# S5 parameter loads beside the output projection, weight slots by time of last use, and the S5 gate ahead of the second half of layer 1's norm

## What is computed

```python
for l in range(2):
    sh1, sc1, g1, sh2, sc2, g2 = split(silu(c) @ ada_w[l] + ada_b[l])   # 1024 x 6144 weights
    h = rms_norm(x) * (1 + sc1) + sh1
    if l == 0:                     # z = h @ w_in (1024 x 3368); A: differential attention, 4 heads
        y = concat(A(z), B(z)) @ w_out                 # B: top-64 sparse attention with an indexer
    else:                          # z = h @ w_in (1024 x 2048); C: causal attention, 8 heads
        s = gelu(s5_scan(u, lam, B, C, D, log_dt))     # D: S5 state-space layer on u, 512 channels
        y = concat(C(z), s * sigmoid(s @ glu_w + glu_b)) @ w_out
    x = x + g1 * y
    h = rms_norm(x) * (1 + sc2) + sh2
    x = x + g2 * hier_moe(h)       # 4 groups, top-2 of 32 experts; w1, w3, w2 of all experts are read
```

## Time and profile before

| | |
|---|---|
| median of 3 runs | 1529.83 us (1529.28 to 1530.37) |
| the profiled execution | 1531.76 us, span 1530.0 us |
| busy: PE, DVE, ACT, POOL | 86%, 28%, 14%, 7% |
| layer 0's mixer, routing included | 0 to 309.57 us |
| layer 0's experts | 309.57 to about 786 us |
| layer 1's mixer, routing included | to 1046.1 us |
| layer 1's experts and output | to the end |
| HBM read | 489.25 MB |

### The profile page before, as it was taken

The page is one execution under the profiler, slowest core; times in us unless marked ns, Lnnn a source line. Parts: engine busy times, 40 slices in busy tenths (PEclk is TensorE's granted clock), DMA queues, the critical chain, the costliest instruction groups (busy, mean ns, idle before and its releaser), DMA issues.

```text
span 1530.0 us, 15107 instructions
## 1 busy us (share of the span) xinstructions
PE 1322.5 (86%) x6157; PEld 662.5 (43%) x6157; DVE 431.4 (28%) x888; ACT 217.9 (14%) x458; POOL 105.6 (7%) x128
## 2 busy tenths in 40 slices
PE   5889989699989988988967865978999899899897
PEld 2334468544334433433435323875343343343333
DVE  3164663721111111110135715253211111111112
ACT  1123241111101110110100004211111010110100
POOL 1110000300300300300000000000000000000000
PEclk8999959699999999999988977779999999999999
DMA  9998521159999999999991097113999999999993
GB/s 371 222 371 344 205 125 55 55 213 430 428 429 427 427 429 427 429 427 428 428 399 63 1 377 310 49 61 116 420 428 428 428 428 426 428 428 428 428 427 159
DMA packets 51801, 493.46 MB, mean 323 GB/s; under 512 B 4744, under 2 KB 5968, under 8 KB 20880
## 3 DMA queue, kind: packets, MB, share of 16 engines
q1 hardware_dynamic: 48816, 488.33, 76.8%
q0 software_dynamic: 1056, 0.89, 1.2%
q10 hardware_dynamic: 1856, 3.20, 0.6%
HBM read 489.25 MB, written 3.15 MB: 322 GB/s over the span
## 4 chain that ended last, share of the span: by engine, by line
PE 48%; DMA 39%; DVE 7%; issue 2%; ACT 2%; SPq 1%; DVEq 0%; POOLq 0%; POOL 0%; PEldq 0%; ACTq 0%
DMA ring<-in_moe_w 34%; PE B L735 19%; PE B L572 5%; PE A L652 4%; PE B L752 3%; PE B L585 3%; DMA ring<-in_ev_w_in 2%; PE B L707 2%; PE B L529 2%; DMA ring<-in_ada_w 2%; PE A L762 2%; PE B L518 2%; PE B L622 1%; PE B L951 1%; DVE work L1030 1%
## 5 line engine op out<-in xcount | busy, mean ns | idle before, releaser
L735 PE MATMUL B<-ring,work 128*64 128x512 f32 x2048 | 475.4, 618 | 62.6 <-DMA ring<-in_moe_w 60.3
L735 PEld LDWEIGHTS B<-ring,work 128*64 128x64 f32 x2048 | 159.5, 142 | 340.5 <-issue 339.1
L752 PE MATMUL B<-ring,work 128*64 128x512 f32 x1024 | 231.8, 594 | 1.2 <-ACT work L1678 1.2
L1301 DVE TENSOR_TENSOR work<-work,B 64x512 f32<-64x512 f32 x64 | 68.1, 1065 | 506.8 <-ACT work L1674 506.3
L752 PEld LDWEIGHTS B<-ring,work 128*64 128x64 f32 x1024 | 75.9, 137 | 137.2 <-issue 137.2
L1674 ACT ACTIVATE work<-B 64x512 f32<-64x512 f32 x64 | 37.7, 589 | 621.5 <-PE B L735 621.5
L762 PE MATMUL A<-work 128*128 128x256 f32 x512 | 118.1, 384 | 8.9 <-DVE work L1307 8.9
L1885 POOL COPY work<-work 128x512 f32 x62 | 38.2, 617 | 1106.3 <-PE B L735 744.8
L762 PEld LDWEIGHTS A<-work 128*128 128x128 f32 x512 | 94.6, 190 | 28.5 <-issue 16.9
L572 PE MATMUL B<-ring,hT 128*128 128x512 f32 (+1 forms) x224 | 96.8, 593 | 5.6 <-DVE hT L1081 3.3
L1307 DVE COPY work<-B 64x512 f32<-64x512 f32 x64 | 43.7, 684 | 117.4 <-PE B L752 117.4
(11 more groups left out here) (248 smaller groups left out, 940.5 us busy)
## 6 DMA issues: line engine op xcount, KB each, us to landing
ring<-in_moe_w SPq DMA_DIRECT2D x192, 2048.0 KB, 19.9
ring<-in_ada_w SPq DMA_DIRECT2D x24, 2048.0 KB, 20.5
ring<-in_ev_w_in SPq DMA_DIRECT2D x6, 2048.0 KB, 22.0
ring<-in_od_w_in SPq DMA_DIRECT2D x4, 2048.0 KB, 19.4
ring<-in_ev_w_out SPq DMA_DIRECT2D x2, 2048.0 KB, 8.1
ring<-in_od_w_out SPq DMA_DIRECT2D x2, 2048.0 KB, 11.0
s_tables<-hT ACTq DMA_DIRECT2D x8, 256.0 KB, 9.5
ring<-s_tables SPq DMA_DIRECT2D x1, 2048.0 KB, 24.6
```

The costliest lines, as they stand in the source:

```text
L735: ins = pe.matmul(B5[64 * m:64 * m + 64, :], xs[:, k, :], w[:, k, :], start=(k == 0), stop=(k == KD - 1))
L752: ins = pe.matmul(B7[64 * m:64 * m + 64, :], hidTb[:, q % 2, k, :], w[:, k, 512 * m:512 * m + 512], start=(k == 0), stop=(k == KF - 1))
L1301: dve.tensor_tensor(hid[64:128, q % 2, :].rearrange("p (k q) -> p q k", k=KF), silu_a[64:128, q % 2, :].rearrange("p (q k) -> p q k", k=KF ...
```

## The change

1. **Slots.** `stream()` gives a load the slot whose content is used first, with "tab" ranked behind ("in", 3). Eight loads of layer 1's mixer get another predecessor, whose use they wait for: ada 7: ("in", 1) in place of tab; ("in", 3): ada 4 (was ("in", 1)); ada 8: ada 5 (ada 4); ada 9: ("in", 2) (ada 5); ada 10: ada 6 (("in", 2)); ada 11: ada 7 (ada 6); glu: ("in", 3) (ada 7); out 1: tab (("in", 3)). All others keep theirs.
2. **S5 loads.** log_dt is read as one row with the norm gains and broadcast by two small matmuls; lam follows it on GpSimd's queue. The router weights of a layer are issued when its last output projection weights have landed, and B, C, D and glu_b after layer 0's last transposes ahead of attention (A3).
3. **S5 matrices.** The DVE block is now the function `s5_matrices`, called between `out_rows_a` and `residual` of layer 0; the seven passes on PE (`s5_transposes`) and ACT stand between `out_proj(0, 0)` and `moe(0)`. The buffers moved accordingly.
4. **Layer 1's gate.** Gelu is y times sigmoid of twice the argument (one DVE op less), and it and the gate stand ahead: DVE does `s5_rows(3)` and gelu's argument, then `c_norm(0)`, the product `gy`, `c_norm(1)`; PE does the gate matmul after tile 0's transposes, then tile 1's, then all of attention; ACT does gelu's sigmoid, root 9, tile 0's copies, root 10, the gate's sigmoids, tile 1's copies.

```diff
+def used_rank(n):
+
+    return N_MIX1 + LOADS1.index(("in", 3)) + 0.5 if n == N_MIX1 + LOADS1.index(("tab",)) else n
+
+
 def stream():
 
 
     slot, fill, old, last, count = [], [], [], {}, [0] * RING
     for n in range(N_ALL):
-        s = n % RING
+        s = n if n < RING else min(last, key=lambda x: used_rank(last[x]))
...
-                 "ada0r2", "bt0", "bt1", "bt2", "bt3", "ct0", "ct1", "k0", "ada0c2", "B0", "B1", "B2", "B3", "ada1r0", "A0", "A1", "A2", "A3"]
+                 "ada0r2", "ada0c2", "B0", "B1", "B2", "B3", "ada1r0", "A0", "A1", "A2", "A3"]
...
-        ORDER += ["oB0", "oB1", "oA0", "oA1", "h0_0", "h0_1", "h0_2", "h0_3", "ada1r1", "ada1c1", "ada1r2", "ada1c2",
+        ORDER += ["oB0", "oB1", "oA0", "oA1", "bt0", "bt1", "bt2", "bt3", "ct0", "ct1", "k0", "h0_0", "h0_1", "h0_2", "h0_3", "ada1r1", "ada1c1", "ada1r2", "ada1c2",
...
+                for g in range(2):
+                    ins = pe.matmul(A4[64 * g:64 * g + 64, 2, 0:16], ones[0:1, 0:64], prow[:, PROWS - 32 + g:PROWS:2], start=True, stop=True)
...
+            def s5_transposes():
+
+                for v in range(4):
+                    tr_unit(f"bt{v}", [Bd[:, v, 4 * q4:4 * q4 + 4, :].rearrange("p a b -> p (a b)") for q4 in range(4)],
+                            [(p5_bt, 1)])
+                for v in range(2):
+                    tr_unit(f"ct{v}", [Cd[:, v, q4, :] for q4 in range(4)])
+                direct_term()
...
                 if q == 4:
-                    for v in range(4):
-                        tr_unit(f"bt{v}", [Bd[:, v, 4 * q4:4 * q4 + 4, :].rearrange("p a b -> p (a b)") for q4 in range(4)],
-                                [(p5_bt, 1)])
-                    for v in range(2):
-                        tr_unit(f"ct{v}", [Cd[:, v, q4, :] for q4 in range(4)])
-                    direct_term()
                     ada_columns(0, 2)
...
+            s5_transposes()
             moe(0)
...
-            def gate(j):
-                if j != GATE_AT:
-                    return
-                for h in range(2):
-                    tr_unit(f"C{2 + h}", [z1[:, 1, 512 * h + P * b:512 * h + P * b + P] for b in range(4)], [(qk_ready, 8)])
+            def gate():
                 n = n_of(1, "glu")
                 pe.wait_ge(gy_ready, 1)
                 full(n)
@@ -995,10 +1001,12 @@
                 ins.then_inc(glu_done, 1)
                 pe.wait_ge(glu_done, 1)
                 pe.nop().then_inc(slot_used, 1)
-                pe.wait_ge(tr_ev, U["C3"] + 1)
-
-            pe.wait_ge(tr_ev, U["C1"] + 1)
-            attention(1, N0, L1_UNITS, gate)
+
+            gate()
+            for h in range(2):
+                tr_unit(f"C{2 + h}", [z1[:, 1, 512 * h + P * b:512 * h + P * b + P] for b in range(4)], [(qk_ready, 8)])
+            pe.wait_ge(tr_ev, U["C3"] + 1)
+            attention(1, N0, L1_UNITS)
...
+            def s5_matrices():
+
+                dve.wait_ge(in_s5, 16 * N_S5)
...
+                tell(p5_bt)
...
             out_rows_a(1, 16)
+            s5_matrices()
             residual(0, 0)
...
-            c_norm(0)
             s5_rows(3)
             dve.wait_ge(y5_read, 4)
 
             w0 = vv[:, 0]
             tt(w0, y5, y5, ALU.mult)
             ts(w0, w0, 0.044715, 1.0, ALU.mult, ALU.add)
-            dve.tensor_tensor(w0, w0, y5, ALU.mult).then_inc(tanh_in, 1)
+            dve.tensor_tensor(w0, w0, y5, ALU.mult).then_inc(gelu_in, 1)
+            c_norm(0)
+            dve.wait_ge(gelu_out, 1)
+            dve.tensor_tensor(gy, w0, y5, ALU.mult).then_inc(gy_ready, 1)
             c_norm(1)
-            dve.wait_ge(tanh_out, 1)
-            ts(w0, w0, 0.5, 0.5, ALU.mult, ALU.add)
-            dve.tensor_tensor(gy, w0, y5, ALU.mult).then_inc(gy_ready, 1)
...
+            act.wait_ge(par_rows, 1)
+            act.activation(s5p[:, 2, :], A4[:, 2, 0:16], ACT.Exp).then_inc(p5_dt, 1)
...
             norm_root(1)
+            for v in range(4):
+                tr_evac(f"bt{v}", BT[:, v // 2, v % 2], 4)
+            for v in range(2):
+                tr_evac(f"ct{v}", CT[:, v], 4)
+            tr_evac("k0", K0[:, :, :].rearrange("p a b -> p (a b)").unsqueeze(1), 1)
             moe(0)
...
+            act.wait_ge(gelu_in, 1)
+            act.activation(vv[:, 0], vv[:, 0], ACT.Sigmoid, scale=2.0 * GELU_C).then_inc(gelu_out, 1)
             root(9, small[:, 0:16])
-            for t in range(TT):
-                if t:
-                    act.wait_ge(tanh_in, 1)
-                    act.activation(vv[:, 0], vv[:, 0], ACT.Tanh, scale=GELU_C).then_inc(tanh_out, 1)
-                    root(10, small[:, 0:16])
-                for h in range(2):
-                    tr_evac(f"C{2 * t + h}", qkT1[:, 4 * h:4 * h + 4, P * t:P * t + P], 4)
-            def gate(j):
-                if j == GATE_AT + 1:
-                    act.wait_ge(in_late, 16 * N_LATE)
-                    act.wait_ge(glu_done, 1)
-                    for f in range(4):
-                        ins = act.activation(vv[:, 1, f, :], OB[f // 2][:, TOK * (f % 2):TOK * (f % 2) + TOK], ACT.Sigmoid, bias=glub[:, f:f + 1])
-                    ins.then_inc(sig_ready, 1)
-
-            attention(N0, L1_UNITS, sc_sb1, prob1, PT1, gate)
+            for h in range(2):
+                tr_evac(f"C{h}", qkT1[:, 4 * h:4 * h + 4, 0:P], 4)
+            root(10, small[:, 0:16])
+            act.wait_ge(in_s5, 16 * N_S5)
+            act.wait_ge(glu_done, 1)
+            for f in range(4):
+                ins = act.activation(vv[:, 1, f, :], OB[f // 2][:, TOK * (f % 2):TOK * (f % 2) + TOK], ACT.Sigmoid, bias=glub[:, f:f + 1])
+            ins.then_inc(sig_ready, 1)
+            for h in range(2):
+                tr_evac(f"C{2 + h}", qkT1[:, 4 * h:4 * h + 4, P:2 * P], 4)
+
+            attention(N0, L1_UNITS, sc_sb1, prob1, PT1)
...
-            pool.wait_ge(h_ready, 2)
+            for dst, src, slow in LAM_PARAMS:
+                pool.dma_start(dst, src, allow_slow_non_contiguous=slow).then_inc(in_lam, 16)
+
+            def router_parameters(l):
+
+                n = n_of(l, "out", 0)
+                pool.wait_ge(slot_full[slot(n)], fills(n))
+                for dst, src, slow in ROUTER_PARAMS[l]:
+                    pool.dma_start(dst, src, allow_slow_non_contiguous=slow).then_inc(in_router[l], 16)
+
+            router_parameters(0)
+            pool.wait_ge(tr_ev, U["A3"] + 1)
             for dst, src, slow in S5_PARAMS:
                 pool.dma_start(dst, src, allow_slow_non_contiguous=slow).then_inc(in_s5, 16)
-            pool.wait_ge(z_ready, 6)
-            for dst, src, slow in LATE_PARAMS:
-                pool.dma_start(dst, src, allow_slow_non_contiguous=slow).then_inc(in_late, 16)
...
+                else:
+                    router_parameters(1)
```

More of the change, by code:

```diff
@@ L624, in att_pv, with attention @@
                 ins.then_inc(pv_done, 1)
-            def attention(l, base, units, hook):
+            def attention(l, base, units, hook=None):
                 n = len(units)
@@ L866, in _ @@
                     ada_rows(0, 1)
-                    tr_unit("lam", [s5row[:, :]], [(in_s5, 16 * N_S5)])
+                    tr_unit("lam", [s5row[:, :]], [(in_lam, 16 * len(LAM_PARAMS))])
                 if q == 2:
@@ L1651, in att_pt, with attention @@
                 tr_evac(f"p{base + j}", pt[:, (base + j) % 2, 0:nb, :], nb)
[L1653 removed]
+            def attention(base, units, buf, pr, pt, hook=None):
                 n = len(units)
```

104 lines of the change are left out of this document (48 added, 56 removed).

## The result

The changed kernel takes 1484.95 us (median of 4, 1482.93 to 1486.34) against 1529.55 us (4 runs, 1528.52 to 1530.37): ratio 0.9709, 95% interval 0.9694 to 0.9725. The profiled execution took 1486.34 us, its span is 1484.5 us. The forecast was 1488.6 us, with a range of 1482 to 1499; the gain is 44.6 us against 41.2 on record.

The account below looks back on a forecast made before the run. Expert stages run at the pace of weight loads, so time ended earlier in mixers and routing counts in full: 18.2 + 23.0 = 41.2 us off 1531.76 gives 1490.6; the median lies 1.93 lower, 1488.6 us, range 1482 to 1499.

Parts of the forecast that it names:

- The early wait: Layer 0's mixer: without early parameter loads, PE's third chunk starts at 72.6 in place of 84.46, -11.8 us.
- the third chunk: Layer 0's mixer: the chunk takes 13.97 us in place of 15.70 when PE comes straight from work, -1.7 us.
- The passes: Layer 0: seven S5 passes on PE leave the place between chunks 4 and 5, -5.3 us.
- The overshoot of the S5 block: Layer 0: the moved DVE block outlasts DVE's wait before the residual, delaying PE, +0.6 us (0 to 2.1).
- Rival B: Layer 0: the early wait stays, as the ring's loads are slow for another reason; 1502 us, chance 10%.
- Rival D: Layer 0: S5's loads land late, holding up DVE's residual, norm and routing; slower than before, 1541 us at 110 us, chance 2%.
- ada 7's wait: Layer 1's mixer: its load is issued earlier, so project1(4) starts at 876.3 in place of 894.48, -18.2 us.
- Rival C: Layer 1: loads of ada 9 to 11 come late and a new wait replaces the removed one; 1494 to 1499 us, chance 8%.
- the order: Layer 1: reordering around the gate shortens 31.3 us from last adaLN copy to first attention values to 28.3, -3.0 (-5 to +1).
- past V nothing is altered: Layer 1: behind the first attention values the change was taken to alter nothing, with 484 us from the experts to the end.
- Rival A: Layer 0: small matmuls in PE's hole before routing keep its clock full; -4.4 us, 1484 us, chance 15%.
- The rule on tables: ACT, layer 1's gate: a skill rule adds some 1.38 us drain per table switch; the forecast charged only 1.28 per load.

Follow-up runs that it names:

- b_dtrow: The kernel before with one load altered, log_dt as one row broadcast by two small matmuls: 1514.37 us, ratio 0.9901 to the kernel before.
- a_dt: The changed kernel with log_dt's two element by element loads put back early, into unread room: 1505.74 us, ratio 0.9849 to the kernel before.
- a_gate: The changed kernel with the old order around layer 1's gate put back: 1481.13 us, ratio 0.9697 to the kernel before.
- g_warm2: a_warm2 with the old order around layer 1's gate: 1474.11 us, ratio 0.9628 to the kernel before.
- E1: Not a run but a point in each profile, layer 1's first expert matmul: at 1046.10 us in the kernel before, 1002.05 in the changed kernel.
- b_slots: The kernel before with only the choice of slots by time of last use: 1505.03 us, ratio 0.9854 to the kernel before.
- a_warm2: The changed kernel with clearing matmuls of zeros in the hole of the norm and routing's two holes: 1473.69 us, ratio 0.9629 to the kernel before.
- a_bc: The changed kernel with B's and C's loads added back early, into unread room: 1490.57 us, ratio 0.9753 to the kernel before.

## Why the prediction was right

**Layer 0, forecast -18.2, profile -19.8.** The early wait and the third chunk gave -12.3 and -1.7 for -11.8 and -1.7 (the four adaLN groups took 7.07 us as one piece, where I had 4 x 1.92). The passes gave -5.3: the first scores moved from 187.25 to 167.90, which is 19.35, less 12.3 and 1.7. The overshoot of the S5 block, +0.6, didn't come: DVE was 1.4 us quicker with it, and started at 225.33. Rival B (the wait stays) falls by b_dtrow and a_dt. Rival D (the S5 loads land late) was far off: they landed within 17.6 us of issue, in the shadow of attention.

**Layer 1, forecast -23.0, profile -24.2.** ada 7's wait: project1(4) from 894.48 to 856.47, less the 19.9 us that P moved, is 18.1, for 18.2; its length fell by 1.76, for 1.8. Rival C (late loads next in line) didn't come: behind it PE waits for no load up to the gate. Up to V the order gave 3.2 us, for 3.0 (28.90 us from the adaLN transposes at 881.99, and 32.07 before), with the table load at 1.28 us and the activation 0.01 behind it (below). But as a term of the time it isn't seen. The whole less the two halves without it is -0.4 or 1.0 us, with 5 to either side; undoing it cost -0.5 us in a_gate, with 4 to either side, and -0.2 or so in g_warm2, with 5. None of the three excludes 3.0 us by itself; taken together as independent they give about 0 with 2.7 to either side (an estimate), which leaves 3.0 just outside. The profiles say why: from P to E1 it is 194.1 us with the new order and 194.4 in b_slots without it. The step at fault is the sentence that past V nothing is altered; the clock in attention and in the output projection comes back at another time.

So the total was in part luck. Without that term the forecast would have been 1491.6 us, some 7 above the median, and even the lowest bounds that the forecast gives for its terms add up to 1486.6 us only, above the measured 1484.95. The range held it because it reached down to the price of rival A, which didn't come. In the profile the time below the forecast has these sources: 1.6 us in layer 0 (0.5 early, the 0.6 of S5's overshoot, 0.5 behind), 1.1 behind V in layer 1, and 1.5 from E1 to the end (482.45 us for 483.9). The last is within what equal programs show there (482.5 to 484.1).

**Rival A** had 15% and did not come in the changed kernel. Its mechanism is real, and its price of 4.4 us for layer 0 about right: a_warm2's logits give 3.4 and the transposes behind them 0.9 (1.07 us for 1.95). The packing gives 1.7 more there, and logits and packing 3.4 + 2.8 in layer 1, which the forecast left out. What it had wrong is the condition: the 56 small matmuls and transposes end at 256.6, and between the next transposes and the logits PE waits 2.28 us with nothing to do.

**The rule on tables.** Timeline of ACT in the changed kernel:

```profile
882.87 1.28 ACT L1829 ACT_TABLE_LOAD   x1
884.16 1.06 ACT L1829 ACTIVATE work<-work 128x1024 f32<-128x1024 f32 x1
885.24 1.28 ACT L1641 ACT_TABLE_LOAD   x1
886.53 0.21 ACT L1641 ACTIVATE small<-small 128x16 f32<-128x16 f32 x1
```

Two loads in a row and no gap at either. The drain of some 1.38 us a switch of the Trainium skill, "ScalarE: Activation LUTs" (What ACT_TABLE_LOAD costs), isn't in these rows. The Trainium skill's rule on DMAs that the forecast names, "DMA: Bandwidth & Descriptors" (Rules for kernel authors), to issue a DMA early and to wait for it late, didn't hold for these loads. Early, log_dt element by element cost 15.1 us (b_dtrow), and B and C some 8 (a_bc, in good part unexplained).

## What to carry to other kernels

Look at the DMA engines' share by queue before the bytes: two loads of together 8 KB in 2048 elements took 16 us of all engines from the weight loads of 2 MB, and one row with a broadcast by matmul cost nothing to be seen. Where a wait is on a slot and not on the bandwidth, its gain can be summed from the rows (20.0 us forecast, 19.9 found). Where matmuls stand behind a hole of PE, read the granted clock at them: if it's at half, other matmuls moved into the hole can bring them back to full clock. In a_warm2 the stretches with such holes are 10.3 us shorter in the profile, for 64 matmuls of zeros in layer 0 and 80 in layer 1, of which 16 each were needed anyway.
